# Up products of the second block's MLP: one 512-column matmul for both halves of the features, VectorE adds the two halves of the bank, and ScalarE takes Relu and both squares one product later

## The chip, the cores and the metric

The kernel runs on one core of one Trainium2 chip. The metric is the device time of one execution in microseconds; lower is better. TensorE (PE in the profile) does the matmuls, VectorE (DVE) and ScalarE (ACT) prepare operands and take results out of PSUM, SyncE (SP) issues the weight transfers.

## The reference

Two transformer blocks run one after the other on 256 tokens of width 1024. The change touches only the last part of the second block, its MLP with a squared Relu:

```python
D_MODEL, SEQ, D_FF = 1024, 256, 4096

def sq_relu_mlp(h, w_up, w_down):
    return jnp.square(jax.nn.relu(h @ w_up)) @ w_down

def second_block(x, norm1_g, ..., norm2_g, w_up, w_down):
    ...
        h = rms_norm_2(x, norm2_g[l])
        x = x + sq_relu_mlp(h, w_up[l], w_down[l])
    return x
```

## The kernel before

All matmuls of this part are products of float32 values that are split in two. A value v becomes a high part (a copy of v to the type fp32r) and a low part (v minus the high part, again fp32r). A product is the sum of three passes: high weights by high features, high weights by low features, low weights by high features.

**The up products.** `w_up` is cut in 32 chunks of 1024 x 128 (512 KB, half of one DMA into a slot of `ring`). Chunk g gives product g: 128 of the 4096 hidden units on the partitions, 256 tokens in the columns of PSUM bank `g % 4`. The features lie in `hfh` (high) and `hfl` (low), each eight blocks of 128 x 256. `product` (lines 480, 481, 484) issues 24 matmuls of 256 columns: for each of eight blocks k one with `hfh` and one with `hfl` against the same high weights, then eight of the low weights with `hfh`. Products 0 and 1 are cut in two halves (`up_rows`, lines 992, 993, 996), since the second half of the features arrives later.

**The chunks.** A chunk n of weights needs a high and a low part before TensorE can take it. ScalarE makes the high one (`hi(n)`, line 1045, 128 x 1024), VectorE the low one (`lo(n)`, line 1512, 128 x 1024). There are NB = 3 pairs of buffers, `half_0` to `half_5`, so `hi(n)` waits until the product three chunks earlier is done. Both engines work two chunks ahead of TensorE. The first pass of a product waits for `hi(n)`, its last eight matmuls for `lo(n)`.

**The square.** After product g ScalarE writes `rl[g % 3]` = Relu(bank) (line 1499), VectorE squares it in place (line 2239), ScalarE copies it to `gh` as the high part (line 1501), and VectorE writes `gl_` = rl - gh (line 2232), one product later. `gh` and `gl_` are the stationary operands of the down products.

The order on each engine is written out by hand, and every instruction waits its turn. For product g ScalarE runs `hi(g+2)`, Relu(g), then the copy to `gh` once VectorE has squared; VectorE runs `lo(g+2)`, the square of g, then `gl_` of g-1:

```python
for g in range(32):          # ScalarE
    taken("up", g)           # hi(g + 2), then wait for product g
    ...Relu(g)...
    e.wait_ge(s_gsq, 5 + g)  # VectorE's square of g
    ...gh(g)...
for g in range(32):          # VectorE
    lo(chunk_at["up", g] + 2)
    ...wait for Relu(g), square(g), gl_(g - 1)...
```

**The down products** (lines 1019 to 1021) follow at once: for each of 32 chunks of `w_down` twelve matmuls of 512 columns into banks 4 to 7, with the same `hi` and `lo` two chunks ahead. When they are done, VectorE adds the result to `xs` (line 2252) and SP writes it out.

Of the kernel before, what the change touches and what calls it, by code (L numbers as in the profile page):

```python
# [5 lines left out]
f32 = mybir.dt.float32  # L6
bf16 = mybir.dt.bfloat16
f32r = mybir.dt.float32r
u32 = mybir.dt.uint32
ALU = mybir.AluOpType  # L10
AF = mybir.ActivationFunctionType
AX = mybir.AxisListType
# [3 lines left out]
T, D = 256, 1024  # L16
# [114 lines left out]
def build_program(nc, A, out):  # L131
    ctx = ExitStack()

    def sem(name):
        return ctx.enter_context(nc.semaphore(name))
# [6 lines left out]
    chunk_at = {}  # L142
    for n, (name, i, c, kind) in enumerate(chunks):
# [29 lines left out]
        "a2", "lru_in", "gl", "lru_mul", "g_sq", "xo", "neg_max", "norm_bcast_read", "h2_done", "h_gained", "rstd_diag", "first_experts")]  # L173

    s_adc = sem("s_last_adc")
    s_pool, s_flp, s_id, s_const, s_wbd, s_iu = [sem("s_" + n) for n in (
        "pool", "mix_lo", "ident", "consts", "wbd0", "iu")]

# [13 lines left out]
    FLV = counted(("h", 4), ("h3", 4), ("val", 8), ("h4", 4))  # L192
# [84 lines left out]
    def st(name, shape, dt=f32):  # L277
        return stage.enter_context(nc.sbuf_tensor(name, shape, dt))
# [32 lines left out]
    feats = ExitStack()  # L311
# [16 lines left out]


    halves2 = [feats.enter_context(nc.sbuf_tensor(f"half2_{i}", [128, 1024], f32r)) for i in range(2 * NB)]  # L330
    hfh = feats.enter_context(nc.sbuf_tensor("hfh", [128, 8, T], f32r))
    hfl = feats.enter_context(nc.sbuf_tensor("hfl", [128, 8, T], f32r))
    xn3 = feats.enter_context(nc.sbuf_tensor("xn3", [128, 2, D], f32))
    mxh = st("mxh", [128, 8, T], f32r)
    mxl = st("mxl", [128, 8, T], f32r)
# [14 lines left out]
    gh = st("gh", [128, 32, T], f32r)  # L350
    gl_ = st("gl_", [128, 32, T], f32r)
    rl = st("rl", [128, 3, T])
    stage.close()
    ctx.push(feats)

    bada, n1pre, ca_w, cqk_w = pc0[:, 8:56], pc0[:, 56:64], pc0[:, 64:88], pc0[:, 88:120]
    mh_w = pc1[:, 8:16]
# [82 lines left out]
    def ahead(n):  # L440

        return [n + 2] if 0 < n < WQ0 - 2 or WQ0 + 16 <= n < NCH - 2 else []
# [7 lines left out]
    def tensor_program(e):  # L450
        o = Own(s_chunk)
        frees = [()] * 8

        def bank(b):
            for s, v in frees[b]:
                e.wait_ge(s, v)
            return banks[b]
# [15 lines left out]
        def product(name, f, b, xh, xl_, by_k=None):  # L473
            n = chunk_at[name, f]
            hi, lo = high_done(n)
            pb = bank(b)
            for k in range(8):
                if by_k:
                    by_k(k)
                e.matmul(pb[:, 0:256], hi[:, k, :], xh[:, k, :], start=k == 0, stop=False)  # L480
                e.matmul(pb[:, 0:256], hi[:, k, :], xl_[:, k, :], start=False, stop=False)  # L481
            e.wait_ge(s_lov, split(n))
            for k in range(8):
                r = e.matmul(pb[:, 0:256], lo[:, k, :], xh[:, k, :], start=False, stop=k == 7)  # L484
            r.then_inc(*o.inc(s_chunk, n + 1))
# [495 lines left out]
                frees[2 * c + a] = ((s_gsq, 2 * c + a + 1),)  # L981


        def up_rows(f, g):
            n = chunk_at["up", f]
            hi, lo = high_done(n)
            pb = bank(f)
            for k in range(4 * g, 4 * g + 4):
                for a in range(2):
                    e.wait_ge(s_fhi, FHI["h4", 2 * a + g])  # L990
                    e.wait_ge(s_flv, FLV["h4", 2 * a + g])
                e.matmul(pb[:, 0:256], hi[:, k, :], hfh[:, k, :], start=k == 0, stop=False)
                e.matmul(pb[:, 0:256], hi[:, k, :], hfl[:, k, :], start=False, stop=False)
            e.wait_ge(s_lov, split(n))
            for k in range(4 * g, 4 * g + 4):
                r = e.matmul(pb[:, 0:256], lo[:, k, :], hfh[:, k, :], start=False, stop=k == 7)
            return r

        up_rows(0, 0)
        for a in range(2):  # L1000
            tokens_columns(a, 1)
        up_rows(1, 0)
        for f in range(2):
            up_rows(f, 1).then_inc(*o.inc(s_chunk, chunk_at["up", f] + 1))
            frees[f] = ((s_relu, f + 1),)
        for g in range(2, 32):
            product("up", g, g % 4, hfh, hfl)
            frees[g % 4] = ((s_relu, g + 1),)
        accs = [bank(4 + i) for i in range(4)]
        for g in range(32):  # L1010
            hi, lo = split_done(chunk_at["dn", g])
# [15 lines left out]
    def scalar_program(e):  # L1027
        o = Own(s_act)

        def hi(n):  # L1030
            i, v, h, _ = chunk_of(n)
            e.wait_ge(*arrived(i))
            if n == WO0 + 1:
                e.wait_ge(s_flp, FLP["ym", 7])
            elif n == WO0 + 4:
                e.wait_ge(s_mix, 8)
                e.wait_ge(s_fhi, FHI["mix", 7])
                e.wait_ge(s_flp, FLP["mix", 7])
            elif WO0 + 3 <= n < WQ0:
                e.wait_ge(s_chunk, WO0)  # L1040
            elif WQ0 + 16 <= n < WQ0 + 19:
                e.wait_ge(s_chunk, WQ0 + 16)
            elif n >= NB and not WO0 <= n < WQ0:
                e.wait_ge(s_chunk, n - NB + 1)
            e.activation(h, v, AF.Copy).then_inc(*o.inc(s_hi, split(n)))  # L1045

        def taken(name, f):

            n = chunk_at[name, f]
            for m in ahead(n):  # L1050
                hi(m)
            e.wait_ge(s_chunk, n + 1)
# [439 lines left out]
        tokens_square(1)  # L1492


        for g in range(32):
            taken("up", g)
            if g >= 3:
                e.wait_ge(s_flp, FLP["g", g - 3])
            e.activation(rl[:, g % 3, :], banks[g % 4][:, 0:256], AF.Relu).then_inc(*o.inc(s_relu, g + 1))
            e.wait_ge(s_gsq, 5 + g)  # L1500
            e.activation(gh[:, g, :], rl[:, g % 3, :], AF.Copy).then_inc(*o.inc(s_fhi, FHI["g", g]))
        for g in range(32):
            for m in ahead(chunk_at["dn", g]):
                hi(m)

    def vector_program(e):
        o = Own(s_vec)
# [712 lines left out]
        def mean_square_inverse(a):  # L2220

            root_bias(hs[a], "h4", a, SQ["h4", a])
            e.wait_ge(s_nsq, SQ["h4", 2 + a])
            e.wait_ge(*o.now)
            e.scalar_tensor_tensor(out=hs[a][2], in0=hs[a][1], scalar=1.0 / 1024, in1=hs[a][3], op0=ALU.mult,
                                   op1=ALU.add).then_inc(*o.inc())
            e.wait_ge(*o.now)
            e.reciprocal(hs[a][2], hs[a][2]).then_inc(*o.inc())

        def square_lo(g):  # L2230
            e.wait_ge(s_fhi, FHI["g", g])
            e.tensor_tensor(gl_[:, g, :], rl[:, g % 3, :], gh[:, g, :].bitcast(f32), ALU.subtract).then_inc(
                *o.inc(s_flp, FLP["g", g]))


        for g in range(32):
            lo(chunk_at["up", g] + 2)
            e.wait_ge(s_relu, g + 1)
            e.tensor_tensor(rl[:, g % 3, :], rl[:, g % 3, :], rl[:, g % 3, :], ALU.mult).then_inc(*o.inc(s_gsq, 5 + g))
            if g:  # L2240
                square_lo(g - 1)
            if 8 <= g < 10:
                mean_square_inverse(g - 8)
        square_lo(31)
        for g in range(32):
            for m in ahead(chunk_at["dn", g]):
# [168 lines left out]
```

## Time and profile before

| | us |
|---|---|
| median of 3 runs | 1283.15 (1282.66 to 1284.62) |
| the profiled execution, its own time | 1282.77 |
| its span, first to last instruction | 1281.0 |
| up products 2 to 31, first matmul to first matmul of the down products | 1100.35 to 1190.15 |
| down products, first matmul to the start of the last one with low weights | 1190.15 to 1277.2 |

Over the whole span PE is busy 90%, DVE 71%, ACT 39%, and the granted clock is 0.969 of 2.4 GHz on average. The span is a sequence of stages with different limits, so these shares say little about the last 190 us, which are the only part that the change touches. Times in the rows below are microseconds from the start of the span. Matmuls are pipelined: what counts is the distance from one start to the next, not the duration that a row prints.

### The profile page before, as it was taken

The page shows a single profiled execution, that of the slowest core. Times are in us where ns is not written, and L with a number is a line of the kernel's source. Part 1 is how long each engine was busy: PE and PEld are TensorE (multiplying, and loading weights), DVE is VectorE, ACT ScalarE, POOL GpSimd, SP SyncE. Part 2 cuts the span into 40 slices and gives each one's busy share as a digit, 9 for nine tenths or more (in the row PEclk, how much of TensorE's full clock was granted, in tenths as well). Part 3 has the DMA queues.
Part 4 walks back from the last instruction along what each step waited for, and adds up shares of the span by engine and source line. Part 5 has one row for each costly group of instructions (what it writes and reads, how often), then busy time and mean ns, then how long its engine had stood idle before and what let it go on. Part 6 is the DMA issues. An engine that isn't in the chain of part 4 may idle for free.

```text
span 1281.0 us, 15451 instructions
## 1 busy us (share of the span) xinstructions
PE 1153.7 (90%) x5476; PEld 818.1 (64%) x5476; DVE 909.3 (71%) x1849; ACT 500.8 (39%) x963; POOL 333.7 (26%) x311
## 2 busy tenths in 40 slices
PE   5999999999799998997788878777889999999998
PEld 4988999999655544442334433332335887999787
DVE  5975797788779776777667767677756786666544
ACT  3656544455532222212222122221524577555432
POOL 5000000000255545445444544444451000000000
PEclk8899999999899999999989998899899999999999
DMA  9863376686899999999999999999997523445550
GB/s 357 322 254 141 134 287 257 256 340 252 327 425 422 426 425 427 425 426 427 426 426 427 427 426 426 427 426 426 428 419 307 193 99 117 148 172 190 198 197 34
DMA packets 58096, 405.67 MB, mean 317 GB/s; under 512 B 6924, under 2 KB 7124, under 8 KB 9636
## 3 DMA queue, kind: packets, MB, share of 16 engines
q0 software_dynamic: 38576, 272.49, 50.8%
q1 hardware_dynamic: 19444, 132.19, 27.5%
q8 instruction: 44, 0.72, 0.2%
q14 instruction: 32, 0.26, 0.1%
HBM read 403.61 MB, written 1.05 MB: 316 GB/s over the span
## 4 chain that ended last, share of the span: by engine, by line
PE 44%; DMA 33%; DVE 12%; ACT 6%; issue 3%; POOL 1%; SPq 0%; POOLq 0%; DVEq 0%; ACTq 0%
DMA gbuf<-in_peer_uv,ei 17%; PE bank L833 9%; DMA ring<-in_peer_uv,ei 9%; PE bank L480 5%; PE bank L484 5%; PE bank L481 5%; DVE half L1512 4%; DMA row_place<-in_peer_uv,ei 4%; ACT half L1045 3%; PE bank L1019 2%; PE bank L1020 2%; PE bank L1021 2%; PE bank L765 2%; DMA wq_place<-in_peer_uv,ei 2%; PE bank L501 1%
## 5 line engine op out<-in xcount | busy, mean ns | idle before, releaser
L833 PE MATMUL bank<-gbuf,dg 128*128 128x512 f32 x540 | 258.3, 623 | 53.2 <-ACT dg L1324 53.2
L1512 DVE TENSOR_TENSOR half<-ring,half 128x1024 fp32r<-128x1024 f32 x175 | 212.7, 1223 | 112.8 <-ACT half L1045 112.5
L833 PEld LDWEIGHTS bank<-gbuf,dg 128*128 128x128 f32 x540 | 105.1, 199 | 195.6 <-issue 121.7
L1973 DVE CUSTOM_DVE_ANT_0 gbuf<-gbuf,h2t 128x1024 f32<-128x1024 f32 x135 | 165.5, 1226 | 81.8 <-DMA gbuf<-in_peer_uv,ei 80.7
L1045 ACT ACTIVATE half<-ring 128x1024 fp32r<-128x1024 f32 x175 | 182.9, 1052 | 100.2 <-PE bank L1021 45.6
L2319 POOL DMA_INDIRECT gbuf<-in_peer_uv,ei x135 | 165.3, 1224 | 185.9 <-PE bank L833 120.1
L833 PE MATMUL bank<-ring,dg 128*128 128x512 f32 x356 | 174.2, 627 | 32.0 <-ACT dg L1324 32.0
L1316 ACT ACTIVATE za<-za 128x4 f32<-128x4 f32 x62 | 12.7, 205 | 399.7 <-DVE za L1973 399.7
L2319 POOL DMA_INDIRECT ring<-in_peer_uv,ei x89 | 106.1, 1192 | 173.4 <-DVE ei L1946 76.5
L833 PEld LDWEIGHTS bank<-ring,dg 128*128 128x128 f32 x356 | 70.2, 201 | 123.7 <-issue 81.0
L1973 DVE CUSTOM_DVE_ANT_0 ring<-ring,h2t 128x1024 f32<-128x1024 f32 x89 | 108.8, 1224 | 56.0 <-DMA ring<-in_peer_uv,ei 56.0
L480 PE MATMUL bank<-hh,half 128*128 128x256 f32 x448 | 113.5, 290 | 0.6 <-DVE hl L1670 0.3
L481 PE MATMUL bank<-hl,half 128*128 128x256 f32 x448 | 110.9, 285 | 0.0
L1324 ACT ACTIVATE dg<-ident,za 128x128 f32<-128x128 f32 x256 | 82.9, 391 | 37.7 <-DVE za L1984 32.9
L480 PEld LDWEIGHTS bank<-hh,half 128*128 128x128 f32 x448 | 86.8, 194 | 1.5 <-issue 0.8
L481 PEld LDWEIGHTS bank<-hl,half 128*128 128x128 f32 x448 | 86.8, 194 | 0.5 <-issue 0.5
L480 PE MATMUL bank<-hfh,half 128*128 128x256 f32 x304 | 76.6, 290 | 0.0
L481 PE MATMUL bank<-hfl,half 128*128 128x256 f32 x304 | 74.4, 283 | 0.0
L484 PE MATMUL bank<-hh,half 128*128 128x256 f32 x448 | 62.8, 283 | 0.0
L480 PEld LDWEIGHTS bank<-hfh,half 128*128 128x128 f32 x304 | 58.0, 191 | 1.1
L481 PEld LDWEIGHTS bank<-hfl,half 128*128 128x128 f32 x304 | 58.2, 191 | 0.1
L484 PEld LDWEIGHTS bank<-hh,half 128*128 128x128 f32 x448 | 57.8, 192 | 0.0
(437 smaller groups left out, 1940.6 us busy)
## 6 DMA issues: line engine op xcount, KB each, us to landing
ring<-in_weights SPq DMA_DIRECT2D x114, 1024.0 KB, 5.0
gbuf<-in_weights SPq DMA_DIRECT2D x4, 1024.0 KB, 9.9
gbuf<-in_peer_uv,ei POOLq DMA_INDIRECT x135, 23.2
wq_place<-in_weights SPq DMA_DIRECT2D x2, 1024.0 KB, 6.9
bcs<-in_b_ada POOLq DMA_DIRECT2D x3, 512.0 KB, 10.5
ring<-in_peer_uv,ei POOLq DMA_INDIRECT x89, 23.0
xs<-in_x SPq DMA_DIRECT2D x2, 512.0 KB, 4.0
ya<-in_weights SPq DMA_DIRECT2D x1, 1024.0 KB, 17.1
```

Of the source, the lines that this page charges most:

```text
L480: e.matmul(pb[:, 0:256], hi[:, k, :], xh[:, k, :], start=k == 0, stop=False)
L481: e.matmul(pb[:, 0:256], hi[:, k, :], xl_[:, k, :], start=False, stop=False)
L484: r = e.matmul(pb[:, 0:256], lo[:, k, :], xh[:, k, :], start=False, stop=k == 7)
L765: r = e.matmul(pb[:, s_], v[:, k, :], hf[:, k, s_], start=k == 0, stop=k == 7)
L833: r = e.matmul(acc[a][j][:, :], dg[:, i % 4, :], expert_rows(i)[:, 1024 + 512 * j:1536 + 512 * j], start=h == 0 and k == 0, stop=h == 7 an ...
L1019: e.matmul(q, l_h, hi[:, 0, s_], start=g == 0, stop=False)
L1020: e.matmul(q, l_h, lo[:, 0, s_], start=False, stop=False)
L1045: e.activation(h, v, AF.Copy).then_inc(*o.inc(s_hi, split(n)))
L1324: e.activation(dg[:, i % 4, :], ident[:, :], AF.Copy, scale=za[:, i // 16 % 2, 16 + i % 16:17 + i % 16]).then_inc(*o.inc(s_dg, i + 1))
L1512: e.tensor_tensor(l, v, h.bitcast(f32), ALU.subtract).then_inc(*o.inc(s_lov, split(n)))
L1973: e.tensor_tensor_reduce(row, row, h2t[:, ITS[n][0], :], 1.0, 0.0, ALU.mult, ALU.add, za[:, n % 2, i % 16:i % 16 + 1]).then_inc(*o.inc(s_d ...
L2319: e.indirect_dma_start(out=expert_rows(i), out_offset=None, in_=A["peer_uv"], in_offset=bass.IndirectOffsetOnAxis(ap=ei[:, a, at:at + 1], ...
```

## The change

The features' two halves become one tensor `hf2` of 128 x 2 x 8 x 256, so that one matmul of 512 columns reads both halves of block k. Columns 0 to 255 of the bank then hold the high features' sum and columns 256 to 511 that of the low features; the low weights still add 256 columns to the first half. VectorE adds the two halves with a reduction over the pair (it reads the bank as 256 pairs whose members lie 256 columns apart) into `rl`. ScalarE then does Relu in place in `rl`, a square to the new float32 buffer `rq` and a square to `gh`, one product later than before. VectorE subtracts `gh` from `rq` two products later. A bank is free for product g when the sum of product g - 4 is taken.

```diff
-    hfh = feats.enter_context(nc.sbuf_tensor("hfh", [128, 8, T], f32r))
-    hfl = feats.enter_context(nc.sbuf_tensor("hfl", [128, 8, T], f32r))
+    hf2 = feats.enter_context(nc.sbuf_tensor("hf2", [128, 2, 8, T], f32r))
...
+    rq = st("rq", [128, 3, T])
...
+    hfh, hfl = hf2[:, 0, :, :], hf2[:, 1, :, :]
...
-        def up_rows(f, g):
-            n = chunk_at["up", f]
+        def up_rows(f, k0, k1):
+
+            n, pb = chunk_at["up", f], banks[f % 4]
             hi, lo = high_done(n)
-            pb = bank(f)
-            for k in range(4 * g, 4 * g + 4):
-                for a in range(2):
-                    e.wait_ge(s_fhi, FHI["h4", 2 * a + g])
-                    e.wait_ge(s_flv, FLV["h4", 2 * a + g])
-                e.matmul(pb[:, 0:256], hi[:, k, :], hfh[:, k, :], start=k == 0, stop=False)
-                e.matmul(pb[:, 0:256], hi[:, k, :], hfl[:, k, :], start=False, stop=False)
+            for k in range(k0, k1):
+                if f < 2:
+                    for a in range(2):
+                        e.wait_ge(s_fhi, FHI["h4", 2 * a + k // 4])
+                        e.wait_ge(s_flv, FLV["h4", 2 * a + k // 4])
+                e.matmul(pb[:, :], hi[:, k, :], hf2[:, :, k, :], start=k == 0, stop=False)
             e.wait_ge(s_lov, split(n))
-            for k in range(4 * g, 4 * g + 4):
+            for k in range(k0, k1):
                 r = e.matmul(pb[:, 0:256], lo[:, k, :], hfh[:, k, :], start=False, stop=k == 7)
             return r
...
         for g in range(2, 32):
-            product("up", g, g % 4, hfh, hfl)
-            frees[g % 4] = ((s_relu, g + 1),)
+            if g < 4:
+                bank(g)
+            else:
+                e.wait_ge(s_usum, g - 3)
+            up_rows(g, 0, 8).then_inc(*o.inc(s_chunk, chunk_at["up", g] + 1))
...
-        for g in range(32):
-            taken("up", g)
+        def relu_square(g):
+            e.wait_ge(s_usum, g + 1)
+            e.activation(rl[:, g % 3, :], rl[:, g % 3, :], AF.Relu).then_inc(*o.inc(s_relu, g + 1))
             if g >= 3:
                 e.wait_ge(s_flp, FLP["g", g - 3])
-            e.activation(rl[:, g % 3, :], banks[g % 4][:, 0:256], AF.Relu).then_inc(*o.inc(s_relu, g + 1))
-            e.wait_ge(s_gsq, 5 + g)
-            e.activation(gh[:, g, :], rl[:, g % 3, :], AF.Copy).then_inc(*o.inc(s_fhi, FHI["g", g]))
+            e.wait_ge(s_relu, g + 1)
+            e.activation(rq[:, g % 3, :], rl[:, g % 3, :], AF.Square).then_inc(*o.inc())
+            e.activation(gh[:, g, :], rl[:, g % 3, :], AF.Square).then_inc(*o.inc(s_fhi, FHI["g", g]))
+
+        for g in range(32):
+            for m in ahead(chunk_at["up", g]):
+                hi(m)
+            if g:
+                relu_square(g - 1)
         for g in range(32):
             for m in ahead(chunk_at["dn", g]):
                 hi(m)
+            if g == 0:
+                relu_square(31)
...
         def square_lo(g):
             e.wait_ge(s_fhi, FHI["g", g])
-            e.tensor_tensor(gl_[:, g, :], rl[:, g % 3, :], gh[:, g, :].bitcast(f32), ALU.subtract).then_inc(
+            e.tensor_tensor(gl_[:, g, :], rq[:, g % 3, :], gh[:, g, :].bitcast(f32), ALU.subtract).then_inc(
                 *o.inc(s_flp, FLP["g", g]))
...
         for g in range(32):
             lo(chunk_at["up", g] + 2)
-            e.wait_ge(s_relu, g + 1)
-            e.tensor_tensor(rl[:, g % 3, :], rl[:, g % 3, :], rl[:, g % 3, :], ALU.mult).then_inc(*o.inc(s_gsq, 5 + g))
-            if g:
-                square_lo(g - 1)
+            if g >= 3:
+                e.wait_ge(s_fhi, FHI["g", g - 3])
+            e.wait_ge(s_chunk, chunk_at["up", g] + 1)
+            e.tensor_reduce(rl[:, g % 3, :], banks[g % 4][:, :].rearrange("p (j t) -> p t j", j=2), AX.X, ALU.add).then_inc(
+                *o.inc(s_usum, g + 1))
+            if g >= 2:
+                square_lo(g - 2)
             if 8 <= g < 10:
                 mean_square_inverse(g - 8)
+        square_lo(30)
         square_lo(31)
```

On TensorE, the last up product and the first matmul of the down products (half_2 and half_3 are the high and low part of the last chunk). Before:

```order
L480 MATMUL bank<-hfh,half_2 128x256
L481 MATMUL bank<-hfl,half_2 128x256
L480 MATMUL bank<-hfh,half_2 128x256
L481 MATMUL bank<-hfl,half_2 128x256
L484 MATMUL bank<-hfh,half_3 128x256 x8
L1019 MATMUL bank<-half_4,gh 128x512
```

The pair of the first two rows stands there eight times. In the changed kernel, the same place (the order names the new tensor `hf`):

```order
L995 MATMUL bank<-hf,half_2 128x512 x8
L998 MATMUL bank<-hf,half_3 128x256 x8
L1025 MATMUL bank<-half_4,gh 128x512
```

Sixteen matmuls of 256 columns have become eight of 512; the eight of the low weights are as they were.

On VectorE, two turns from the middle of the up products, with the semaphores that each instruction waits for. Before:

```order
L1512 TENSOR_TENSOR half_1<-ring,half_0 128x1024 [waits s_hi]
L2239 TENSOR_TENSOR rl<-rl 128x256 [waits s_relu]
L2232 TENSOR_TENSOR gl_<-rl,gh 128x256 [waits s_feat_hi]
L1512 TENSOR_TENSOR half_3<-ring,half_2 128x1024 [waits s_hi]
L2239 TENSOR_TENSOR rl<-rl 128x256 [waits s_relu]
L2232 TENSOR_TENSOR gl_<-rl,gh 128x256 [waits s_feat_hi]
```

And now:

```order
L1527 TENSOR_TENSOR half_1<-ring,half_0 128x1024 [waits s_hi]
L2256 TENSOR_REDUCE rl<-bank 128x256 [waits s_chunk,s_feat_hi]
L2247 TENSOR_TENSOR gl_<-rq,gh 128x256 [waits s_feat_hi]
L1527 TENSOR_TENSOR half_3<-ring,half_2 128x1024 [waits s_hi]
L2256 TENSOR_REDUCE rl<-bank 128x256 [waits s_chunk,s_feat_hi]
L2247 TENSOR_TENSOR gl_<-rq,gh 128x256 [waits s_feat_hi]
```

The square has gone, and the reduction of the bank has its place; it waits for TensorE (`s_chunk`) and not for ScalarE's Relu of the same product, and `gl_` is that of product g - 2.

On ScalarE, two turns from the same stretch. Before:

```order
L1045 ACTIVATE half_2<-ring 128x1024 [waits s_chunk,s_ring2]
L1499 ACTIVATE rl<-bank 128x256 [waits s_mix_lo,s_chunk]
L1501 ACTIVATE gh<-rl 128x256 [waits s_g_sq]
L1045 ACTIVATE half_4<-ring 128x1024 [waits s_chunk,s_ring2]
L1499 ACTIVATE rl<-bank 128x256 [waits s_mix_lo,s_chunk]
L1501 ACTIVATE gh<-rl 128x256 [waits s_g_sq]
```

And now:

```order
L1051 ACTIVATE half_0<-ring 128x1024 [waits s_chunk,s_ring3]
L1503 ACTIVATE rl<-rl 128x256 [waits s_up_sum]
L1507 ACTIVATE rq<-rl 128x256 [waits s_relu,s_mix_lo]
L1508 ACTIVATE gh<-rl 128x256
L1051 ACTIVATE half_2<-ring 128x1024 [waits s_chunk,s_ring3]
L1503 ACTIVATE rl<-rl 128x256 [waits s_up_sum]
```

The wait for VectorE's square (`s_g_sq`) between Relu and `gh` is gone; the turn begins its small work with a wait for VectorE's sum (`s_up_sum`) of the product before. No table load stands between these rows, nor anywhere from here to the end.

## Rows read from the trace of the kernel before

**Rows 1.** Stretches: PE, PEld, DVE, ACT, POOL busy; granted clock; DMA share; GB/s.

```profile
1100.35:1139.71 39.36, 39.36 (x330) 39.36 (x329) 25.44 (x45) 21.71 (x41) 0.00 (x0) 1.00 0.45 161
1142.60:1187.60 45.00, 45.00 (x363) 44.03 (x362) 28.45 (x45) 24.61 (x47) 0.00 (x0) 1.00 0.48 168
1190.10:1277.20 87.10, 87.05 (x383) 71.70 (x384) 40.80 (x39) 33.63 (x34) 0.00 (x0) 1.00 0.39 137
```

**Rows 2.** Timeline (start, length), PE: low weights' pass of products 2, 15, 16, 26.

```profile
1102.27 1.12 PE L484 MATMUL bank<-hfh,half 128*128 128x256 f32 x8
...
1139.71 1.12 PE L484 MATMUL bank<-hfh,half 128*128 128x256 f32 x8
...
1142.68 1.12 PE L484 MATMUL bank<-hfh,half 128*128 128x256 f32 x8
...
1172.64 1.12 PE L484 MATMUL bank<-hfh,half 128*128 128x256 f32 x8
```

**Rows 3.** Timeline of all engines over one turn, 1138.8 to 1141.8.

```profile
1138.80 0.42 DVE L2239 TENSOR_TENSOR rl<-rl 128x256 f32<-128x256 f32 x1
...
1139.25 0.42 ACT L1501 ACTIVATE gh<-rl 128x256 fp32r<-128x256 f32 x1 [1.36 <-DVE rl L2239]
...
1139.58 1.04 ACT L1045 ACTIVATE half<-ring 128x1024 fp32r<-128x1024 f32 x1
...
1140.52 0.36 ACT L1499 ACTIVATE rl<-bank 128x256 f32<-128x256 f32 x1
1140.65 1.23 DVE L1512 TENSOR_TENSOR half<-ring,half 128x1024 fp32r<-128x1024 f32 x1 [1.10 <-ACT half L1045]
1140.67 0.38 PE L480 MATMUL bank<-hfh,half 128*128 128x256 f32 x1
...
1141.79 0.42 DVE L2239 TENSOR_TENSOR rl<-rl 128x256 f32<-128x256 f32 x1
...
1142.13 0.42 DVE L2232 TENSOR_TENSOR gl_<-rl,gh 128x256 fp32r<-128x256 f32 x1
```

**Rows 4.** Who waited for whom (us, times, longest), 1110 to 1185.

```profile
ACT gh L1501 <- DVE rl L2239: 34.0, 25, 1.4
DVE half L1512 <- ACT half L1045: 26.4, 25, 1.1
```

**Rows 5.** Timeline, PE: down products, two starts 24 matmuls apart.

```profile
1270.12 0.39 PE L1019 MATMUL bank<-half,gh 128*128 128x512 f32 x1
...
1275.57 0.39 PE L1019 MATMUL bank<-half,gh 128*128 128x512 f32 x1
```

**Rows 6.** Timeline, PE and DVE: where product 2 and the down products begin.

```profile
1096.56 0.69 DVE L1555 TENSOR_TENSOR hfl<-bank,hfh 128x512 fp32r<-128x512 f32 x1 [0.63 <-ACT hfh L1075]
...
1097.39 0.35 PE L992 MATMUL bank<-hfh,half 128*128 128x256 f32 x1
...
1100.35 0.28 PE L480 MATMUL bank<-hfh,half 128*128 128x256 f32 x1
...
1190.15 0.47 PE L1019 MATMUL bank<-half,gh 128*128 128x512 f32 x1 [1.42 <-DVE half L1512]
```

**Rows 7.** Groups by line and shape on DVE: two reductions, one reader of PSUM.

```profile
L1942 DVE TENSOR_REDUCE pk<-pk 128x16 f32<-128x256 f32 x30 | 12.6, 420 | 1.0
L2206 DVE TENSOR_TENSOR xs<-xs,bank 128x512 f32<-128x512 f32 x4 | 2.7, 682 | 0.2 <-PE bank L501 0.2
L2097 DVE TENSOR_REDUCE sm<-mixT 128x8 f32<-128x512 f32 x4 | 2.7, 682 | 2.0 <-ACT mixT L1409 2.0
```

**Rows 8.** Timeline, ACT: square (L1070), copy (L1045), Relu (L1499) in sequence.

```profile
1097.03 0.62 ACT L1070 ACTIVATE mixT<-xs 128x512 f32<-128x512 f32 x1
...
1097.64 1.05 ACT L1045 ACTIVATE half<-ring 128x1024 fp32r<-128x1024 f32 x1
1099.11 0.38 ACT L1499 ACTIVATE rl<-bank 128x256 f32<-128x256 f32 x1 [0.42 <-PE bank L996]
```

**Rows 9.** Waits of SP's queue, 1080 to 1281.

```profile
SPq L2380 <- DVE half L1512: 161.5, 29, 10.1
```

More of the change, by code:

```diff
@@ L175, in build_program @@
     s_adc = sem("s_last_adc")
+    s_usum = sem("s_up_sum")
     s_pool, s_flp, s_id, s_const, s_wbd, s_iu = [sem("s_" + n) for n in (
@@ L981, in tensor_program @@
                 frees[2 * c + a] = ((s_gsq, 2 * c + a + 1),)
-        def up_rows(f, g):
-            n = chunk_at["up", f]
+        def up_rows(f, k0, k1):
+            n, pb = chunk_at["up", f], banks[f % 4]
             hi, lo = high_done(n)
-            pb = bank(f)
-            for k in range(4 * g, 4 * g + 4):
-                for a in range(2):
-                    e.wait_ge(s_fhi, FHI["h4", 2 * a + g])
-                    e.wait_ge(s_flv, FLV["h4", 2 * a + g])
-                e.matmul(pb[:, 0:256], hi[:, k, :], hfh[:, k, :], start=k == 0, stop=False)
-                e.matmul(pb[:, 0:256], hi[:, k, :], hfl[:, k, :], start=False, stop=False)
+            for k in range(k0, k1):
[4 more added lines that the diff above has]
+                e.matmul(pb[:, :], hi[:, k, :], hf2[:, :, k, :], start=k == 0, stop=False)
             e.wait_ge(s_lov, split(n))
-            for k in range(4 * g, 4 * g + 4):
+            for k in range(k0, k1):
                 r = e.matmul(pb[:, 0:256], lo[:, k, :], hfh[:, k, :], start=False, stop=k == 7)
             return r
-        up_rows(0, 0)
+        bank(0)
+        up_rows(0, 0, 4)
         for a in range(2):
             tokens_columns(a, 1)
-        up_rows(1, 0)
+        bank(1)
+        up_rows(1, 0, 4)
         for f in range(2):
-            up_rows(f, 1).then_inc(*o.inc(s_chunk, chunk_at["up", f] + 1))
-            frees[f] = ((s_relu, f + 1),)
+            up_rows(f, 4, 8).then_inc(*o.inc(s_chunk, chunk_at["up", f] + 1))
         for g in range(2, 32):
-            product("up", g, g % 4, hfh, hfl)
-            frees[g % 4] = ((s_relu, g + 1),)
+            if g < 4:
[3 more added lines that the diff above has]
+            up_rows(g, 0, 8).then_inc(*o.inc(s_chunk, chunk_at["up", g] + 1))
         accs = [bank(4 + i) for i in range(4)]
```

## The prediction

> **What bounds the kernel now.** The change touches only the last 190 us, so I read no whole-span share, but the stretches first [rows 1]: from 1100 to the end TensorE is busy all the time at the full 2.4 GHz (granted clock 1.00), while DVE is busy for 25.44 of 39.36 us and ACT for 21.71. That looks like a TensorE-bound stage. But a busy PE row is built from overlapping matmuls, so I looked at distances between starts. The low weights' pass of product 2 starts at 1102.27 and that of product 15 at 1139.71: 13 products in 37.44 us, 2.88 us each, or 0.120 us for each of the 24 matmuls. From product 16 to 26 it is 29.96 us for ten, 2.996 each [rows 2]. So something else than the matmuls sets the second half of the stage.
>
> It is a loop between VectorE and ScalarE [rows 3]. VectorE squares at 1138.80; ScalarE's copy to `gh` starts 0.45 later (1139.25), `hi` of the chunk two ahead 0.33 after that (1139.58), VectorE's `lo` 1.07 later (1140.65), and the next square 1.14 later (1141.79). The four steps add up to 2.99, which is the whole turn. None of them waits for TensorE; on the contrary, product 16's first matmul starts at 1140.67, when `hi` at 1139.58 is just done. The table of waits says the same from the other side: in 75 us ScalarE's `gh` waits 25 times for the square, 34.0 us, and VectorE's `lo` 25 times for `hi`, 26.4 us [rows 4]. The loop ran at 2.99 from the beginning, TensorE at 2.88 caught up with it after 14 products. A last effect stands where the stage ends: product 31 would hand over at about 1140.67 + 16 x 2.995 = 1188.6, but the down products start at 1190.15, after an idle time put down to `lo` [rows 6]: 1.6 us, since VectorE is that late with the first chunk of `w_down`.
>
> Behind this the down products run 24 matmuls of 512 columns in 5.45 us, 0.227 each [rows 5]. They are TensorE-bound: 87.1 us for 384 matmuls.
>
> **The change on TensorE.** A product becomes 8 matmuls of 512 columns and 8 of 256. The rows for both forms are at the same clock: 8 x 0.227 + 8 x 0.120 = 1.816 + 0.960 = 2.776 us. Two matmuls of 256 cost 0.240, one of 512 costs 0.227, so the merge alone is worth only 0.104 us per product. This price assumes that a moving operand in two pieces of 256 columns (`hf2[:, :, k, :]`) streams like the one piece of the down products; no row shows such a form. From below it can't be less than the 0.227 of one piece; from above I take the pace of two matmuls, 0.240, since two pieces of 256 is what TensorE reads now. Then the product stays at 2.88.
>
> **The change on VectorE.** The square (0.42 long, 0.34 from start to start: from 1141.79 to 1142.13 in rows 3) goes, a reduction of 128 x 512 from PSUM comes. The nearest rows are a reduction of 128 x 512 from SBUF, 682 ns, one of 128 x 256, 420, and an addition that reads 128 x 512 from PSUM, 682 [rows 7]. I take 0.68, or 0.60 from start to start with the overlap of 0.08 that the square shows. VectorE's turn is then `lo` 1.14 + 0.60 + `gl_` 0.34 = 2.08 us. It stays hidden up to a reduction of 2.776 - 1.48 = 1.30 from start to start.
>
> What the rows leave open is the order of reading. All of the 512-element rows read neighbouring elements; the new reduction takes element t and element t + 256, 1024 bytes apart, in turn. From the two reductions, 256 more elements cost 262 ns, 1.02 each, beside 158 fixed. If a jump cost nothing, 0.68; if each element took twice as long, 158 + 1048 = 1.21 long, 1.13 from start to start, still under 1.30; three times, 1.73 long and 1.65 from start to start, no longer hidden.
>
> The Trainium skill has a rule that speaks against this change ("Advanced Engine Details and Errata", section Memory Cachelines, PSUM Cachelines): PSUM has lines of 8 bytes, two float32 values, and every two consecutive elements should be contiguous for best throughput; it says of matmuls that a non-contiguous pattern slows them significantly. It gives no figure for VectorE and no run here shows one; taken as twice the time per element it would leave the sum below as it is, taken as more it is the slow rival.
>
> **The change on ScalarE.** Per turn now `hi` 0.94 (from its start at 1139.58 to Relu's at 1140.52), Relu 0.42 and a wait for it, 0.03, two squares of 0.33 each from start to start, as the copy to `gh` of the same size costs now [rows 3]: 2.05 us against 2.776. A square, a copy and a Relu follow one another at 1097 with no table load between them [rows 8], and the new order shows none. ScalarE has 0.7 us left per turn.
>
> **The loop afterwards.** The wait inside the turn is gone. When product g ends, ScalarE starts `hi(g+3)` (its buffer is free now), VectorE the reduction of g and `gl_` of g-2, done after 0.94. `lo(g+3)` follows at 1.07 and ends at 2.3; Relu and squares of g run from 1.0 to 2.1. Both are done before product g+1 ends at 2.776. The remaining chain from `hi` to `hi` (1.07, `lo` 1.14, reduction 0.60, Relu 0.45, two squares 0.66: 3.9 us) now closes over two turns, 1.96 per turn. Queued behind the reduction's wait for TensorE are `gl_` of g-2 and `lo(g+3)`; TensorE needs that `lo` two products later, the `gl_` only in the down products. So TensorE sets the pace. The reduction frees the bank, and TensorE waits for it four products later, at no cost. Chunks are used every 2.776 us instead of 2.99, which is slower than the 2.72 (12 x 0.227) at which the down products draw the same 512 KB with the DMA engines 39% busy and SP's queue waiting for VectorE to free a slot, 161.5 us in 29 times [rows 1, 9]: transfers stay ahead. Small work on VectorE at products 8 and 9 is absorbed by its 0.7 us of slack.
>
> **The ends.** TensorE reaches the second halves of products 0 and 1 when the last low features are written (1096.56 + 0.69, the matmul at 1097.39), as before. These two halves shrink by 4 x 0.013 each: product 2 starts at 1100.25 instead of 1100.35 [rows 6]. The first `lo` of the down products is ready early: it follows product 29, two products before it is needed. Behind the last product ScalarE has one more Relu and two squares, and VectorE three `gl_`, before the `lo` of the third down chunk: that ends some 4.0 us after product 31 (`hi` 1.05, small work 1.2, `gl_` 0.4, `lo` 1.2) and is needed after 5.4. If it came 1.4 us later still, it would cost.
>
> **The sum.** Halves of products 0 and 1: 0.10. Products 2 to 15: 14 x (2.88 - 2.776) = 1.46. Products 16 to 31: 16 x (2.995 - 2.776) = 3.50. The idle time before the down products: 1.58. Together 6.64 us. The profiled execution took 1282.77, so 1276.1; the median of the runs is 0.38 above that one: 1276.5 us.
>
> **The rivals.**
> *The reduction becomes the bound (slower).* VectorE runs in order, so a turn is 1.48 plus the reduction. Against the forecast nothing changes up to 1.30. All of the gain is gone where a turn is 2.776 + 6.64/30 = 3.0 us, a reduction of 1.52 from start to start, 1.60 long. At three times the time per element (1.65) the turn is 3.13, 30 x 0.354 = 10.6 us more than the forecast: 1287. At four times, 2.17 from start to start, the turn is 3.65 and the time 1303. For it: pairs 1024 bytes apart, which no row has. Against it: the addition that reads PSUM takes the same 682 ns as the reduction from SBUF [rows 7], so PSUM itself is no brake, and doubling is still free. 11 in 100; another 5 in 100 for a reduction just past 1.30, where part of the gain is left (1277 to 1283).
>
> *The 512-column stream in two pieces is no faster than two matmuls.* The product stays at 2.88; the loop's part and the idle time are still won: 6.64 - 0.10 - 30 x 0.104 = 3.4 us, 1279.7. For it: no row has a moving operand in two pieces. Against it: the jump comes once in 256 columns, and the rows for 256 and 512 columns (0.120 and 0.227) differ by 0.107 for 256 more columns, so 0.013 of each matmul does not depend on its length and goes with the matmul. 6 in 100.
>
> *The loop is still there.* Were the new chain longer than I count, TensorE would catch up with it as now. It would have to reach 2 x 2.776 = 5.55 us over two turns where I count 3.9, for instance through a wait for `gl_` in the middle of ScalarE's turn; that one is three products old. Then the time would be between forecast and no change, about 1280. 3 in 100, and it would be seen as waits of PE for `hi`.
>
> The forecast itself: 75 in 100, with a range of its own from 1275.3 to 1277.5 (the down products may lose their 0.3 us of slow start too; the clock may differ). The range to 1281 takes in the two rivals that win less. A difference of 0.2% is 2.6 us, about what a measurement of this kernel can tell from no change. Faster by more: 75, the stream 5, the loop 2, the mild reduction 4, together 86. Within it: 3. Slower: 11.
>
> **What the profile will show.** If right: the low weights' passes of products 2 to 31 are 2.78 us apart from first to last; the reduction is 0.65 to 1.25 us long; DVE's `lo` no longer waits for `hi` behind a square, both engines wait for PE instead; the first down matmul follows the last up product within 0.3 us, at about 1183.5. Each step fails visibly: a 512-column start distance over 0.23 is the second rival; a reduction over 1.38 long, with PE waiting for `lo` or `hi`, the first; ACT rows with table loads, or PE waits with a short reduction, the third. A down product that waits for `lo` in its first three chunks would show the hand-over mis-timed.

## The result and the profile after

| | before | changed |
|---|---|---|
| median of 5 runs | 1283.15 us | 1277.14 us (1276.01 to 1278.14) |
| profiled execution, own time / span | 1282.77 / 1281.0 | 1277.14 / 1275.4 |
| ratio to before, 95% interval | | 0.9950 (0.9939 to 0.9961) |

The changed kernel is 6.0 us faster, 0.5%; by the interval it is 5.0 to 7.8 us. The forecast was 1276.5 within 1275.0 to 1281.0.

These rows of TensorE in the changed kernel (start, length, instruction) are to be held against [rows 2] and [rows 6]. They show product 2 (line 995 the 512-column matmuls, line 998 the low weights), product 16, the last pass of product 31, and the first matmul of the down products.

```profile
1101.08 2.02 PE L995 MATMUL bank<-hf,half 128*128 128x512 f32 x8
1102.93 1.11 PE L998 MATMUL bank<-hf,half 128*128 128x256 f32 x8
1103.88 2.00 PE L995 MATMUL bank<-hf,half 128*128 128x512 f32 x8
...
1140.19 2.00 PE L995 MATMUL bank<-hf,half 128*128 128x512 f32 x8
...
1183.93 1.12 PE L998 MATMUL bank<-hf,half 128*128 128x256 f32 x8
1184.88 0.40 PE L1025 MATMUL bank<-half,gh 128*128 128x512 f32 x1
```

From product 2 to product 16 it is 39.11 us for 14, and from there to the down products 44.69 for 16: 2.79 each in both parts. The knee of [rows 2], the point where the distance grows from 2.88 to 2.996, is gone, and the down products begin 0.95 after the start of the last pass, which is just its eight matmuls: the idle time of [rows 6] is gone too. The stage from product 2 to the down products takes 83.80 us, where it took 89.80.

The turn itself, on the timeline of all engines (compare [rows 3]):

```profile
1140.19 2.00 PE L995 MATMUL bank<-hf,half 128*128 128x512 f32 x8
1140.45 1.06 ACT L1051 ACTIVATE half<-ring 128x1024 fp32r<-128x1024 f32 x1 [0.61 <-PE bank L998]
1140.46 0.69 DVE L2256 TENSOR_REDUCE rl<-bank 128x256 f32<-128x512 f32 x1 [0.48 <-PE bank L998]
1141.07 0.42 DVE L2247 TENSOR_TENSOR gl_<-rq,gh 128x256 fp32r<-128x256 f32 x1
1141.42 0.40 ACT L1503 ACTIVATE rl<-rl 128x256 f32<-128x256 f32 x1
1141.54 1.23 DVE L1527 TENSOR_TENSOR half<-ring,half 128x1024 fp32r<-128x1024 f32 x1
1141.91 0.42 ACT L1507 ACTIVATE rq<-rl 128x256 f32<-128x256 f32 x1
...
1142.23 0.40 ACT L1508 ACTIVATE gh<-rl 128x256 fp32r<-128x256 f32 x1
```

Product 15 ends, and 0.3 us after the start of the next both engines begin at once, the high part and the sum. Both had been idle for TensorE, 0.61 and 0.48 us. The waits of the stage say it for all turns, in the place of [rows 4]:

```profile
engine line waited for: us in total, times, longest us
ACT half L1051 <- PE bank L998: 18.3, 29, 1.2
DVE rl L2256 <- PE bank L998: 12.6, 26, 0.5
DVE half L1527 <- ACT half L1051: 2.1, 3, 1.5
```

The two engines now wait for TensorE and no longer for each other, but for three waits of the low part for the high part. The sum of the two halves is short, in the view of one tile's instructions (least, median, longest ns):

```profile
L2256 DVE TENSOR_REDUCE rl<-bank x32: 682/692/692, 1099.9 to 1185.2; 128x256 f32<-128x512 f32 x32
```

The 1024-byte jumps from element to element cost VectorE next to nothing: 692 ns, and a sum over the same number of neighbouring elements in SBUF took 682 [rows 7]. No run sums neighbouring elements in PSUM.

One row of stretches was not expected. The granted clock (third column from the end) just before product 2:

```profile
1093.00:1094.00 1.00, 0.45 (x4) 0.42 (x4) 0.99 (x2) 0.00 (x0) 0.00 (x0) 1.00 0.93 164
...
1095.00:1096.00 1.00, 1.00 (x5) 1.00 (x6) 0.53 (x1) 0.01 (x1) 0.00 (x0) 0.50 1.06 442
1096.00:1097.00 1.00, 1.00 (x3) 0.74 (x3) 0.38 (x1) 1.00 (x2) 0.00 (x0) 0.50 0.11 41
1097.00:1098.00 1.00, 1.00 (x5) 0.87 (x4) 0.31 (x1) 1.00 (x5) 0.00 (x0) 0.50 0.00 0
```

TensorE runs at 1.2 and not 2.4 GHz for some 3 us, after two idle times of 1.17 and 0.69 us for the last features. Product 2 starts at 1101.08, where 1100.25 was forecast and 1100.35 was measured before the change. Experiments 1, 4 and 8 are about this.

### The profile page after: what moved, and what is told of

Its sections match the earlier page's. It is cut to its first block, busy times and chain, and to the rows that moved or that the text cites. A ratio compares the mean times of both kernels' runs of the same rounds, so it can differ in the third digit from the quotient of the medians.

```text
span 1275.4 us, 14998 instructions
## 1 busy us (share of the span) xinstructions
PE 1151.2 (90%) x5220; PEld 805.1 (63%) x5220; DVE 920.1 (72%) x1849; ACT 515.1 (40%) x995; POOL 333.6 (26%) x311
## 4 chain that ended last, share of the span: by engine, by line
PE 54%; DMA 30%; DVE 8%; issue 3%; ACT 3%; POOL 1%; SPq 0%; POOLq 0%; DVEq 0%; ACTq 0%
DMA gbuf<-in_peer_uv,ei 14%; PE bank L835 11%; DMA ring<-in_peer_uv,ei 11%; PE bank L482 5%; PE bank L486 5%; PE bank L483 5%; PE bank L995 5%; DMA wq_place<-in_peer_uv,ei 4%; PE bank L767 2%; PE bank L998 2%; PE bank L1027 2%; PE bank L1026 2%; PE bank L1025 2%; PE bank L503 1%; DMA ya<-in_weights 1%
## 5 line engine op out<-in xcount | busy, mean ns | idle before, releaser
L2338 POOL DMA_INDIRECT gbuf<-in_peer_uv,ei x135 | 162.2, 1202 | 188.4 <-PE bank L835 119.4
L995 PE MATMUL bank<-hf,half 128*128 128x512 f32 x256 | 65.5, 397 | 0.1
L995 PEld LDWEIGHTS bank<-hf,half 128*128 128x128 f32 x256 | 46.5, 191 | 8.7 <-issue 0.5
L1025 PE MATMUL bank<-half,gh 128*128 128x512 f32 x128 | 49.8, 389 | 0.0
L1026 PE MATMUL bank<-half,gh 128*128 128x512 f32 x128 | 49.8, 389 | 0.0
```

The costliest lines, as they stand in the source:

```text
L995: e.matmul(pb[:, :], hi[:, k, :], hf2[:, :, k, :], start=k == 0, stop=False)
L1025: e.matmul(q, l_h, hi[:, 0, s_], start=g == 0, stop=False)
L1026: e.matmul(q, l_h, lo[:, 0, s_], start=False, stop=False)
L2338: e.indirect_dma_start(out=expert_rows(i), out_offset=None, in_=A["peer_uv"], in_offset=bass.IndirectOffsetOnAxis(ap=ei[:, a, at:at + 1], ...
```

## The experiments

All times are medians; each ratio is to the kernel before, measured beside the experiment. Where a distance between products is given, it is between starts of the same line on TensorE.

**1. The changed kernel again.** No edit.

> The changed kernel once more, with a fresh profile. In its first profile the granted clock falls to 0.50 from about 1094.9 to 1098.2 us, just before product 2, and product 2 starts 0.8 us later than forecast (1101.08, not 1100.25); in the kernel before it stays at 1.00 there. Theory A, the change causes the fall (its first half product is shorter, so TensorE is idle sooner): the fall is there again, time about 1277. Theory B, chance of that one execution: the clock is 1.00 there and the profiled execution is about 1.2 us shorter than the first one, under 1276. The distance between products is 2.79 in both cases.

Measured: 1276.11 us, ratio 0.9951 (0.9937 to 0.9965), span 1274.3. Product 2 starts at 1099.99, at full clock:

```profile
1094.00:1099.00 5.00, 4.20 (x25) 3.47 (x24) 2.74 (x5) 3.52 (x8) 0.00 (x0) 1.00 0.43 179
```

and the down products at

```profile
1183.79 0.40 PE L1025 MATMUL bank<-half,gh 128*128 128x512 f32 x1
```

which is again 83.80 us after product 2. Theory B: the fall of the clock belonged to one execution. The span is 1.1 us shorter without it; the profiled execution took 1276.03, where under 1276 was expected. What the fall cost can be read from the last transposes before the stage (line 463) to product 2. In the first profile they begin at

```profile
1094.87 1.09 PE L463 MATMUL bank<-ident,xn 128*128 128x128 f32 x4 [0.69 <-DVE xn L1557]
```

and here at

```profile
1094.98 0.63 PE L463 MATMUL bank<-ident,xn 128*128 128x128 f32 x4 [0.70 <-DVE xn L1557]
```

so it is 6.21 us to product 2 there and 5.01 here: the fall cost 1.2 us. It does not explain every slower execution. The profiled ones of experiments 6 and 9 took 1277.12 and 1277.28 with a granted clock of 1.00 all through this stretch. In experiment 9 the last transposes begin only at 1096.20, so that execution was 1.2 us behind experiment 1's before it came here; where it lost that time stays open.

**2. The high weights in two matmuls again.**

```diff
-                e.matmul(pb[:, :], hi[:, k, :], hf2[:, :, k, :], start=k == 0, stop=False)
+                if k == 0:
+                    e.matmul(pb[:, :], hi[:, k, :], hf2[:, :, k, :], start=True, stop=False)
+                    continue
+                e.matmul(pb[:, 0:256], hi[:, k, :], hfh[:, k, :], start=False, stop=False)
+                e.matmul(pb[:, 256:512], hi[:, k, :], hfl[:, k, :], start=False, stop=False)
```

> The changed kernel, but for seven of the eight blocks of a product the high weights meet the high and the low features in two matmuls of 256 columns (each into its half of the bank) and not in one of 512. Orders and waits of VectorE and ScalarE are those of the changed kernel. Theory A, the gain is mostly the broken loop and only to a small part the merge: products 2.79 + 7 x 0.01 = 2.86 to 2.88 us apart from first to last, no catching up at product 16, 30 x 0.08 = 2.4 us slower than the changed kernel: 1279.5. Theory B, the merge is what pays: the time is that of before, about 1283.

Measured: 1278.60 us, ratio 0.9965 (0.9953 to 0.9977).

```profile
1101.88 1.12 PE L1002 MATMUL bank<-hf,half 128*128 128x256 f32 x8
...
1185.20 1.12 PE L1002 MATMUL bank<-hf,half 128*128 128x256 f32 x8
1186.16 0.40 PE L1029 MATMUL bank<-half,gh 128*128 128x512 f32 x1
```

29 products in 83.32 us, 2.873 each. Undoing seven of the eight merges costs 0.080 us per product, 0.011 per merge, and 2.4 us in all from the first matmul of product 2 (1099.96) to the down products. Without these merges the kernel is still 4.5 us faster than before by the ratio (3.0 to 6.0): Theory A.

**3. The loop opened in another way, with no merge and no sum.** The kernel before, with

```diff
-            e.wait_ge(s_gsq, 5 + g)
-            e.activation(gh[:, g, :], rl[:, g % 3, :], AF.Copy).then_inc(*o.inc(s_fhi, FHI["g", g]))
+            e.wait_ge(s_relu, g + 1)
+            e.activation(rq[:, g % 3, :], rl[:, g % 3, :], AF.Square).then_inc(*o.inc())
+            e.activation(gh[:, g, :], rl[:, g % 3, :], AF.Square).then_inc(*o.inc(s_fhi, FHI["g", g]))
```

on ScalarE, where Relu also comes before the wait for `gl_` of g-3 and not behind it. VectorE has no square, and takes `rq` in the place of `rl` for `gl_`.

> The kernel before, with its 24 matmuls of 256 columns and Relu straight from the bank, but ScalarE takes both squares itself right after Relu (a square to a float32 buffer, a square to gh) and VectorE no longer squares; there is no sum of halves. Nothing on ScalarE waits for VectorE any more within a turn. Theory A (loop between VectorE and ScalarE was the limit): products 2.88 us apart from first to last, and the down products start 0.3 us after the last product: 1.84 + 1.5 = 3.3 us faster than before, 1279.8. Theory B (the gain needs the merged matmul): no faster than before, 1283.

Measured: 1279.68 us, ratio 0.9975 (0.9963 to 0.9986).

```profile
1101.83 1.12 PE L485 MATMUL bank<-hfh,half 128*128 128x256 f32 x8
...
1185.35 1.12 PE L485 MATMUL bank<-hfh,half 128*128 128x256 f32 x8
1186.31 0.40 PE L1020 MATMUL bank<-half,gh 128*128 128x512 f32 x1
```

29 products in 83.52, 2.880 each to the end, and no gap before the down products: Theory A, 1279.8 expected. By the ratio the gain is 3.2 us (1.8 to 4.7). From the last pass of product 2 to the down products it is 84.48 us; it was 1190.15 - 1102.27 = 87.88 before [rows 2, 6] and is 1184.88 - 1102.93 = 81.95 in the changed kernel. So of the 5.93 us 3.40 come from the opened loop. The other 2.53 are the merge: 29 products, each 2.793 and not 2.880 us.

**4 and 8. Matmuls in the idle times before product 2.**

```diff
         for a in range(2):
+            pb, w = bank(5 + 2 * a), chunk_of(chunk_at["up", 0])[2]
+            for _ in range((8, 4)[a]):
+                e.matmul(pb[:, 0:256], w[:, 0, :], hfh[:, 0, :], start=True, stop=True)
             tokens_columns(a, 1)
```

> The changed kernel with 12 more matmuls of 256 columns that compute nothing used, into banks 5 and 7: eight before the transposes of the second half of the features for tokens 0 to 127 and four before those for tokens 128 to 255, where TensorE is idle for 1.17 and 0.69 us. Theory A (the fall of the clock before product 2 follows from those idle times and costs): clock 1.00 there, product 2 starts about 1.2 us earlier against the stage before it, time 1276.0, a ratio to the changed kernel of 0.999. Theory B (the fall is chance or costs nothing): time as the changed kernel, 1277.

> The kernel with the twelve idle-time matmuls once more, for its spread. The changed kernel's ten times so far lie at 1276.0 to 1276.5 (five) and 1277.1 to 1278.1 (five), those with the filler at 1275.95 to 1276.38 (five of five). Theory A (the clock falls before product 2 in about half of the executions and the filler keeps it up): all times under 1276.6. Theory B (the narrow spread was luck): about half of them over 1277.

Measured: 1276.26 us (1275.95 to 1276.38), ratio 0.9946 (0.9932 to 0.9960); again, 1276.57 (1275.61 to 1277.00), ratio 0.9946 (0.9932 to 0.9959). Experiment 4 looked like a narrower spread; experiment 8 took most of that back: two of its five times are above the 1276.6 of its Theory A, and none is above 1277.0, so neither of its theories was met. The intervals lie on those of the changed kernel. The clock was 1.00 before product 2 in all profiles with the filler, but also in seven of eight without it (the changed kernel's two and experiments 2, 3, 5, 6, 7 and 9). Of the 15 executions with the filler (experiments 4, 8 and 10) one is above 1277.0 us, of 20 without it (the changed kernel, experiments 1, 6 and 9) eight are. That is a hint and no more: experiments 6 and 9 have slower executions whose clock did not fall here. So a benefit of the filler is not shown, and what makes the clock fall in one profile of eight stays open.

**5. Relu and squares in the same turn.**

```diff
         for g in range(32):
             for m in ahead(chunk_at["up", g]):
                 hi(m)
-            if g:
-                relu_square(g - 1)
+            relu_square(g)
...
-            if g == 0:
-                relu_square(31)
```

> The changed kernel, but ScalarE takes Relu and squares of product g in the same turn as the sum of g, behind the high part of chunk g+2, not one product later. The matmuls are those of the changed kernel. Theory A (the one product of delay is what opens the loop): the chain high part 1.07, low part 1.14, sum 0.61, Relu 0.49, two squares 0.65 closes in one turn again, 3.96 to 4.0 us a turn where TensorE needs 2.79: 30 x 1.2 = 35 us slower than the changed kernel, about 1312, and slower than before. Theory B (fewer matmuls and no square on VectorE are enough): about 1277.

Measured: 1317.81 us, ratio 1.0271 (1.0255 to 1.0286), with exactly the matmuls of the changed kernel. The timeline of one turn:

```profile
1151.48 1.23 DVE L1524 TENSOR_TENSOR half<-ring,half 128x1024 fp32r<-128x1024 f32 x1 [1.92 <-ACT half L1051]
1151.59 2.09 PE L995 MATMUL bank<-hf,half 128*128 128x512 f32 x8 [1.04 <-ACT half L1051]
1152.62 0.68 DVE L2253 TENSOR_REDUCE rl<-bank 128x256 f32<-128x512 f32 x1
...
1153.34 0.42 ACT L1503 ACTIVATE rl<-rl 128x256 f32<-128x256 f32 x1 [1.89 <-DVE rl L2253]
...
1154.48 1.04 ACT L1051 ACTIVATE half<-ring 128x1024 fp32r<-128x1024 f32 x1
1155.55 1.22 DVE L1524 TENSOR_TENSOR half<-ring,half 128x1024 fp32r<-128x1024 f32 x1 [1.91 <-ACT half L1051]
```

Low part to low part: 4.07 us, and TensorE stands idle for 1.04 of them for the high part. The loop of [rows 3] is back with a longer chain. Theory A, and 6 us more than expected. The turns alone give what was expected: from the low weights' pass of product 2 (1102.08) to that of product 31 (1218.95) it is 35.9 us more than in the changed kernel, where 35 was worked out. Another 2.7 us is the idle time for VectorE's low part before the down products:

```profile
1222.57 0.71 PE L1025 MATMUL bank<-half,gh 128*128 128x512 f32 x1 [2.51 <-DVE half L1524]
```

The last 2.5 us lie in the down products (93.03 against 90.52 from their first matmul to the end of the span). Most of that is the clock, which was granted in full until this idle time and then fell to 1.2 GHz for some 3 us:

```profile
1224.00:1225.00 1.00, 1.00 (x4) 0.81 (x3) 0.00 (x0) 1.00 (x2) 0.00 (x0) 0.50 0.00 0
```

The first eight matmuls of the down products take 3.48 us (to 1226.05) instead of 1.8. The kernel before had a shorter idle time at this place, 1.42 us [rows 6], and its clock stayed at 1.00.

**6 and 7. The sum done twice and three times.**

```diff
+            for i in range(1):    # range(2) in experiment 7
+                e.tensor_reduce(rj[:, (2 * g + i) % 8, :], banks[g % 4][:, :].rearrange("p (j t) -> p t j", j=2), AX.X,
+                                ALU.add).then_inc(*o.inc())
             e.tensor_reduce(rl[:, g % 3, :], banks[g % 4][:, :].rearrange("p (j t) -> p t j", j=2), AX.X, ALU.add).then_inc(
                 *o.inc(s_usum, g + 1))
```

`rj` is a scratch tensor that nobody reads.

> The changed kernel with VectorE's sum of the halves done twice for each product, the first time to a scratch tensor that nobody reads. VectorE's turn becomes 1.14 + 2 x 0.61 + 0.34 = 2.70 us. Theory A (TensorE sets the pace at 2.79 and VectorE is hidden up to a sum of 1.30): no difference from the changed kernel, 1276 to 1277. Theory B (VectorE's work is on the path, for instance because each turn begins with its wait for TensorE): slower by 30 x 0.61 = 18 us or a good part of it.

> The changed kernel with VectorE's sum of the halves done three times for each product, twice to a scratch tensor. VectorE's turn becomes 1.14 + 3 x 0.61 + 0.34 = 3.31 us and passes TensorE's 2.79. Theory A (the slow rival of the prediction, its threshold at 1.30): products 3.31 us apart once TensorE has caught up, 30 x 0.52 = 15.5 us slower than the changed kernel, about 1292. Theory B (two turns of slack absorb it): under 1280.

Twice: 1276.73 us, ratio 0.9949 (0.9936 to 0.9963), as the changed kernel. Product 2 at 1101.09, down products at 1184.89: 83.80 us, unchanged to the last digit, with 0.6 us more work per turn.

```profile
1101.09 2.00 PE L996 MATMUL bank<-hf,half 128*128 128x512 f32 x8
...
1184.89 0.40 PE L1026 MATMUL bank<-half,gh 128*128 128x512 f32 x1
```

Three times: 1293.65 us, ratio 1.0085 (1.0069 to 1.0100), slower than before the change. VectorE's turn is 3.26 (1151.36 to 1154.62), and TensorE waits for the low part:

```profile
1151.36 1.22 DVE L1528 TENSOR_TENSOR half<-ring,half 128x1024 fp32r<-128x1024 f32 x1
...
1152.63 1.22 PE L999 MATMUL bank<-hf,half 128*128 128x256 f32 x8 [0.21 <-DVE half L1528]
...
1154.62 1.22 DVE L1528 TENSOR_TENSOR half<-ring,half 128x1024 fp32r<-128x1024 f32 x1
```

Theory A in both. One more sum is free, two are not: the slow rival of the prediction is real, and its threshold lies between 1.2 and 1.8 us of sums. The prediction's 1.30 is within these bounds. For three sums the stage from product 2 (1100.31) to the down products (1198.66) grows by 14.6 us (98.35 against 83.80), which includes an idle time of 2.35 us for VectorE's low part at its end. The down products take 2.3 us more (92.84 against 90.52). As in experiment 5 the clock falls behind that idle time: it is 0.50 from 1200 to 1203, and the seven matmuls from 1199.97 to 1202.96 take 2.99 us instead of 1.6.

**9 and 10. The 512 columns in one contiguous piece, without and with the filler.**

```diff
-    hf2 = feats.enter_context(nc.sbuf_tensor("hf2", [128, 2, 8, T], f32r))
+    hf2 = feats.enter_context(nc.sbuf_tensor("hf2", [128, 8, 2, T], f32r))
...
-    hfh, hfl = hf2[:, 0, :, :], hf2[:, 1, :, :]
+    hfh, hfl = hf2[:, :, 0, :], hf2[:, :, 1, :]
...
-                e.matmul(pb[:, :], hi[:, k, :], hf2[:, :, k, :], start=k == 0, stop=False)
+                e.matmul(pb[:, :], hi[:, k, :], hf2[:, k, :, :], start=k == 0, stop=False)
```

> The changed kernel with the features stored as 128 x 8 x 2 x 256, so that the 512 columns of a matmul are one contiguous piece and not two pieces 8 KB apart. In the changed kernel the 512-column matmuls start 0.230 us apart, those of the down products 0.227. Theory A (the jump between the two pieces costs the difference): 0.227 apart, products 2.77 us apart, 0.6 us faster, about 1276.0. Theory B (the difference comes from something else, such as the change between matmuls of 512 and 256 columns): 2.79 as before, about 1276.6.

> The contiguous features together with the twelve idle-time matmuls: the best version that the runs so far point to. Theory A of both: product distance 2.77, no execution in which the clock falls before product 2: median 1275.7, highest under 1277. Theory B: as the changed kernel, median 1276.6.

Measured: 1276.82 us, ratio 0.9949 (0.9935 to 0.9962), and 1276.05 (1275.86 to 1277.11), ratio 0.9947 (0.9933 to 0.9960). In experiment 9:

```profile
1101.24 2.02 PE L995 MATMUL bank<-hf,half 128*128 128x512 f32 x8
...
1185.05 0.40 PE L1025 MATMUL bank<-half,gh 128*128 128x512 f32 x1
```

83.81 us for 30 products, 2.794 each: Theory B. A moving operand in two pieces costs the same as in one. The median of experiment 10 lies between its two theories, and its highest time is above the 1277 of Theory A. Neither version is distinguishable from the changed kernel.

## Why the prediction was right

**The bound.** Right, and shown: from product 16 on the loop between VectorE and ScalarE set the pace, not the matmuls, though TensorE looked busy throughout. Experiment 3 opens the loop and touches no up matmul: 2.880 to the end, where it was 2.996. Experiment 5 closes a loop again, with fewer matmuls: 4.07. The loop was forecast to give 3.4 us and gave 3.40 in experiment 3's rows.

**TensorE's price.** The mechanism was right, the size a little off. A product costs 2.793, not 2.776, so the merge gives 0.087 and not 0.104, 2.6 instead of 3.1 us. A matmul of 256 columns takes 0.119, as before (0.95 for eight, from 1183.93 to 1184.88); one of 512 takes 0.230 (1.84 for eight, from 1140.19 to 1142.03), where the down products' row had 0.227. The form of the operand, which the prediction named as the unknown, is not the cause (experiment 9). By the prediction's own mark, over 0.23, this is just short of its second rival, but the merge did pay, 0.087 of 0.104.

The term that was too small is the 0.227. It comes from the end of the down products [rows 5], a long row of 512-column matmuls, and the changed kernel's own down products do not begin at that price:

```profile
1184.88 0.40 PE L1025 MATMUL bank<-half,gh 128*128 128x512 f32 x1
...
1186.27 0.39 PE L1025 MATMUL bank<-half,gh 128*128 128x512 f32 x1
...
1187.63 0.39 PE L1025 MATMUL bank<-half,gh 128*128 128x512 f32 x1
```

The first six take 1.39 us, 0.232 each, the next six 1.36, 0.227, and it stays at that. Experiments 1, 2, 3 and 9 show the same step after six, experiment 3 too, whose up products have no 512-column matmul. The eight of a product are always the first behind matmuls of 256 columns, so they are paid at about the price of such a start. Why a start is slower no run here tells.

**VectorE's price.** 0.68 was taken and 0.692 measured. The rule against the change, the Trainium skill's "Advanced Engine Details and Errata", section Memory Cachelines, PSUM Cachelines, would have neighbouring elements in PSUM pairwise contiguous for best throughput and speaks of a significant slowdown of matmuls otherwise. For VectorE's read the trace does not agree: 692 ns with every element 1024 bytes from the last, 682 for a contiguous sum in SBUF. What it says of matmuls no run here tests. The threshold beyond which it would have been the slow rival holds within the bounds that experiments 6 and 7 set.

**ScalarE and the order.** Relu to the first square takes 0.49 and not 0.45, and the turn 2.18 and not 2.05, which leaves 0.61 us idle per turn where 0.7 was forecast. No table load appears. The hand-over went as worked out: `lo` of the third down chunk starts at 1187.70 and ends about 4.05 us after product 31; it is needed after 5.4, and TensorE shows no wait there.

**The sum.** The stage from product 2 gave 6.00 us where 6.54 was forecast, and the 0.5 is the price of the 512-column matmul. The down products gave 0.33 that only the range allowed for: from their first matmul to the end of the span it was 90.85 us and is 90.52. These two errors have opposite signs and partly cancel. The second halves of products 0 and 1 take 2.88 us in experiment 1 (1097.11 to 1099.99) and took 2.96: 0.08 where 0.10 was forecast. In the first profile product 2 came 0.73 us later than before, because of the clock, and the span shrank by 5.6; in experiment 1 it came 0.36 earlier, and the span shrank by 6.7. Medians: 6.0 measured, 6.6 forecast.

## What to carry to other kernels

A stage whose TensorE row is full can still be set by two other engines that take turns: measure the distance between equal passes at its start and at its end, and look for a knee. If engine A waits for B and B for A inside one turn, add up the chain around the loop. Opening it was worth more here (3.4 us) than dropping a third of the matmul instructions of a product (2.5 us). Taking a consumer one turn later lets the same chain close over two turns, and in this kernel putting it back cost 41 us. Work on an engine that has slack is free only up to a threshold that can be worked out beforehand, and doubling, then tripling the piece in question finds on which side one is.

## What the runs showed of the hardware that was not expected

- VectorE sums pairs of float32 values 1024 bytes apart in PSUM about as fast as contiguous ones in SBUF: 692 against 682 ns for 512 elements.
- A moving operand of 512 columns in two pieces 8 KB apart streams like one contiguous piece: 2.793 and 2.794 us per product.
- Behind 256-column matmuls the first six distances of 512-column ones are 0.232 us, from there on 0.227. In the up products, which never have more than eight in a row, they are 0.230. The cause is open.
- In one of eight profiles without the filler the granted clock fell to 0.50 for about 3 us after idle times of 1.17 and 0.69 us, and the same idle times in experiment 1 (1.17 and 0.70) left it at 1.00. After idle times of 2.51 and 2.35 us it fell to 0.50 in experiments 5 and 7, for about 3 us each.
